# Three up bodies with 258 columns, the rest on rows of 256, and arrays on multiples of 512 bytes

## What is computed

```python
mod_x = (jax.nn.silu(c) @ w_mod[l] + b_mod[l])[:, None, :]
sh1, sc1, g1, sh2, sc2, g2 = jnp.split(mod_x, 6, axis=-1)
...
xs = xs + g2 * sq_relu_mlp(rms_norm(xs, norm_mlp_g[l]) * (1 + sc2) + sh2, mlp_w1[l], mlp_w2[l])

def rms_norm(x, g):
    y = xf * lax.rsqrt(jnp.mean(xf * xf, axis=-1, keepdims=True) + EPS)
    return (y * g.astype(F32)).astype(x.dtype)

def sq_relu_mlp(h, w1, w2):
    return jnp.square(jax.nn.relu(h @ w1)) @ w2
```

## Time and profile before

| | |
|---|---|
| median of 3 runs | 1370.04 us (1368.95 to 1371.89) |
| profiled execution | 1371.54 us, span of its core 1369.7 us |
| busy | PE 98%, PEld 93%, DVE 62%, ACT 51%, POOL 21% |
| mean granted clock of PE | 0.997 of full speed |
| HBM | 168 MB read, 124 GB/s over the span |

### The profile page before, as it was taken

How to read it: one execution, slowest core, us unless ns; L and a number is a source line. 1 busy time by engine, 2 the same in 40 slices (tenths; PEclk the granted TensorE clock), 3 DMA queues, 4 the chain that set the end, 5 groups by cost and what they waited for, 6 DMA issues and landing times.

```text
span 1369.7 us, 28118 instructions
## 1 busy us (share of the span) xinstructions
PE 1344.8 (98%) x11256; PEld 1269.9 (93%) x11256; DVE 854.4 (62%) x1308; ACT 701.6 (51%) x1135; POOL 287.9 (21%) x296
## 2 busy tenths in 40 slices
PE   6999999999999999999999999999999999999998
PEld 4899998988899999999999999999998988999998
DVE  4755789985455665543587666566736666765563
ACT  4468888878544455422533322333226665663553
POOL 2000224223566786621100000000020000200002
PEclk9999999999999999999999999999999999999999
DMA  9732232322401110123466565565423320656562
GB/s 327 201 87 85 79 92 78 94 78 77 139 33 34 61 33 32 63 78 101 139 193 193 184 194 190 185 192 182 134 93 123 98 74 32 192 175 204 173 194 78
DMA packets 138030, 170.88 MB, mean 125 GB/s; under 512 B 10912, under 2 KB 121760, under 8 KB 137920
## 3 DMA queue, kind: packets, MB, share of 16 engines
q1 hardware_dynamic: 137312, 169.13, 39.4%
q0 software_dynamic: 608, 0.19, 0.1%
HBM read 168.25 MB, written 1.05 MB: 124 GB/s over the span
## 4 chain that ended last, share of the span: by engine, by line
PE 84%; DVE 7%; ACT 4%; issue 2%; POOL 2%; DMA 1%; SPq 0%; DVEq 0%; ACTq 0%; POOLq 0%
PE bank L2531 54%; PE bank L2538 7%; PE bank L2945 3%; PE bank L2933 3%; DVE qkv L1721 2%; DVE w_lo L1655 2%; PE bank L2457 1%; PE bank L2962 1%; POOL qkv L768 1%; PE bank L3184 1%; PE bank L2887 1%; PE bank L3207 1%; PE bank L2911 1%; PE bank L2809 1%; DMA first_w<-in_w_mod 1%
## 5 line engine op out<-in xcount | busy, mean ns | idle before, releaser
L1655 DVE TENSOR_TENSOR w_lo<-raw,w_hi 128x1024 fp32r<-128x1024 f32 x214 | 267.3, 1250 | 308.9 <-ACT w_hi L915 308.4
L915 ACT ACTIVATE w_hi<-raw 128x1024 fp32r<-128x1024 f32 x214 | 225.5, 1055 | 378.0 <-PE bank L2531 376.0
L2531 PE MATMUL bank<-h_hi,w_hi 128*128 128x256 f32 x1472 | 300.0, 282 | 7.4 <-DVE w_lo L1655 4.9
L2531 PE MATMUL bank<-h_hi,w_lo 128*128 128x256 f32 x1472 | 292.8, 277 | 0.0
L2531 PE MATMUL bank<-h_lo,w_hi 128*128 128x256 f32 x1472 | 287.5, 278 | 0.0
L2531 PEld LDWEIGHTS bank<-h_hi,w_hi 128*128 128x128 f32 x1472 | 225.5, 188 | 18.1 <-issue 10.2
L2531 PEld LDWEIGHTS bank<-h_hi,w_lo 128*128 128x128 f32 x1472 | 225.1, 188 | 0.0
L2531 PEld LDWEIGHTS bank<-h_lo,w_hi 128*128 128x128 f32 x1472 | 222.0, 188 | 0.3 <-DVE h_lo L1914 0.2
L2531 PE MATMUL bank<-hid_hi,w_hi 128*128 128x256 f32 x768 | 173.5, 280 | 0.0
L2531 PE MATMUL bank<-hid_hi,w_lo 128*128 128x256 f32 x768 | 172.2, 278 | 0.0
L2531 PE MATMUL bank<-hid_lo,w_hi 128*128 128x256 f32 x768 | 172.2, 278 | 0.0
(11 more groups left out here) (363 smaller groups left out, 2484.7 us busy)
## 6 DMA issues: line engine op xcount, KB each, us to landing
raw<-in_mlp_w SPq DMA_DIRECT2D x128, 512.0 KB, 3.7
late_w<-in_w_mod SPq DMA_DIRECT2D x56, 512.0 KB, 4.4
raw<-in_even_w_in SPq DMA_DIRECT2D x48, 512.0 KB, 3.7
raw<-in_w_mod SPq DMA_DIRECT2D x24, 512.0 KB, 4.4
first_w<-in_w_mod SPq DMA_DIRECT2D x16, 512.0 KB, 10.8
raw<-in_even_w_out SPq DMA_DIRECT2D x16, 512.0 KB, 3.5
raw<-in_attn_w_qkv SPq DMA_DIRECT2D x16, 512.0 KB, 3.7
raw<-in_attn_w_o SPq DMA_DIRECT2D x8, 512.0 KB, 3.5
```

The source lines that it names most:

```text
L915: act.activation(stored(w_hi, j, four), raw[:, j % RAW], ACT.Copy).then_inc(hi_ready, 1)
L1655: dve.tensor_tensor(stored(w_lo, j, four), raw[:, j % RAW], stored(w_hi, j, four).bitcast(F32), ALU.subtract).then_inc(split_done, 1)
L2531: return pe.matmul(bank[2 * pair + t][:, c - n0:c - n0 + CTX], w_[:, k, t * P:(t + 1) * P], x_[:, c:c + CTX], start=(kk == 0 and first and ...
```

## The change

Three edits:

- `up_x`, `rooted_hi`, `rooted_lo` are new. DVE's `normal` makes x · gain · root for one feature tile in one of four buffers, ACT's `normal_high` adds the shift and rounds, and `normal_low` on DVE takes the rest. All eight tiles are made in bodies 0 and 1 of up10 (`NORMAL_IN` = 2), two with each pair.
- Bodies 0 to 2 of up10 (`ROOTLESS` = 3) go on with 258 columns of `up_hi`, `up_lo`, and are written out. Body 3 of up10 and all of up11 multiply `rooted_hi`, `rooted_lo`, 256 columns. There DVE's `positive` takes the maximum with 0 straight from the bank, and ACT only squares. PE waits once for the last `rooted_lo` ahead of body 3.
- `xT`, `raw`, `w_hi`, `w_lo`, and with them `w_hi2`, `w_lo2` and all that `F` places, start on multiples of 512 bytes. The small arrays lie ahead of them; `d_last` moves into `sp_x`.

```diff
+ALIGNED = 512
-SHIFT, UP_ROW = 2, 272
+SHIFT, UP_ROW, ROOTLESS, NORMAL_IN = 2, 272, 3, 2
...
+        base[0] = (base[0] + ALIGNED - 1) // ALIGNED * ALIGNED
+        xT = place("xT", [KT, T])
+        raw = place("raw", [RAW, UNIT_K, UNIT_C])
+        w_hi = place("w_hi", [SPLIT, UNIT_K, UNIT_C], F32R)
+        w_lo = place("w_lo", [SPLIT, UNIT_K, UNIT_C], F32R)
         mod_off = base[0]
...
+        up_x = F("up_x", 76, [4, T - CTX])
+        rooted_lo = F("rooted_lo", 80, [KT, T - CTX], F32R)
+        rooted_hi = F("rooted_hi", 88, [KT, T - CTX], F32R)
...
+                def normal_high(k):
+                    act.wait_ge(nrm["t"], 5 * KT + k + 1)
+                    act.activation(rooted_hi[:, k], up_x[:, k % 4], ACT.Identity, bias=modv[:, 1, 3, k, 1:2]).then_inc(nrm["high"], 1)
...
                 def body(it):
                     u = it * 2 * s["upp"] + s["unit"]
                     for pair in range(2):
                         split_hi(u + 4 + 2 * pair, 4 + 2 * pair, True)
-                        relus(it, pair)
-                        squares_of(it, pair)
+                        squares_alone(it, pair)
...
+            def positive(s, it, pair):
+                dve.wait_ge(hid_done, it * 4 + (s["up"] + 2 * pair + 2))
+                dve.sem_inc(act_waits, 1)
+                dve.wait_ge(slot_free, it * 2 * s["upp"] + (s["unit"] + (pair + 1) * s["upp"] + PRIME_SLOT))
+                for t in range(2):
+                    dve.tensor_scalar(relu[:, 2 * pair + t, 0:T - CTX], bank[2 * pair + t][:, 0:T - CTX], 0.0, None,
+                                      ALU.max).then_inc(evac_done, 1)
+
+            def normal(k):
+                dve.scalar_tensor_tensor(out=up_x[:, k % 4], in0=xT[:, k, CTX:T], scalar=gain[:, 1, 1, k, 1:2],
+                                         in1=n_rs[:, 0:T - CTX], op0=ALU.mult, op1=ALU.mult).then_inc(nrm["t"], 1)
+
+            def normal_low(k):
+                dve.wait_ge(nrm["high"], high_upto(turn["mlp1"], k) + KT)
+                dve.scalar_tensor_tensor(out=rooted_lo[:, k], in0=up_x[:, k % 4], scalar=modv[:, 1, 3, k, 1:2],
+                                         in1=rooted_hi[:, k].bitcast(F32), op0=ALU.add, op1=ALU.subtract).then_inc(nrm["lo"], 1)
...
+                def rootless_body(it):
+                    u = it * 2 * s["upp"] + s["unit"]
+                    for pair in range(2):
+                        k = 4 * it + 2 * pair
+                        if it < NORMAL_IN:
+                            normal(k)
+                            normal(k + 1)
+                        split_lo(u + 4 + 2 * pair, 4 + 2 * pair, True)
+                        rooted(s, it, pair)
+                        if it < NORMAL_IN:
+                            normal_low(k)
+                            normal_low(k + 1)
+                        split_lo(u + 5 + 2 * pair, 5 + 2 * pair, True)
+                        hidden_low(s, it, pair)
...
-                if n0 == 0 and (h is up_hi or h is up_lo):
+                if s["name"] in ("up10", "up11"):
                     kk = j % s["upp"] * UNIT_K + k
+                    n = T - CTX + (SHIFT if h is up_hi or h is up_lo else 0)
...
+                        first = 0
+                        if half == 0:
+                            first = ROOTLESS
+                            for n in range(1, ROOTLESS * per_body):
+                                unit(s_, n // per_body, n % per_body, up_hi, up_lo, 0, **(normed(nm) if n < per_body else {}))
+                            pe.wait_ge(nrm["lo"], high_upto(turn[nm], KT - 1) + KT)
+                        with nc.Fori(first, s_["bodies"], engines=[ENG.PE]) as it:
+                            for n in range(per_body):
+                                unit(s_, it, n, rooted_hi, rooted_lo, 0)
```

More of the change, by code:

```diff
@@ L207, in build @@
         vec = place("vec", [NVEC])
-        xT = place("xT", [KT, T])
-        raw = place("raw", [RAW, UNIT_K, UNIT_C])
-        w_hi = place("w_hi", [SPLIT, UNIT_K, UNIT_C], F32R)
-        w_lo = place("w_lo", [SPLIT, UNIT_K, UNIT_C], F32R)
         modv = place("modv", [2, 6, 8, 2])
@@ L1462, in squares_of, with squares_alone @@
                         act.activation(r_, r_, ACT.Square).then_inc(s_sq, 1)
+                def squares_alone(it, pair):
+                    for t in range(2):
+                        wait_alone(evac_done, it * 4 + (2 * s["pair"] + 2 * pair + t + 1 + PRIME_EVAC))
+                        r_ = relu[:, 2 * pair + t, 0:T - CTX]
+                        act.activation(r_, r_, ACT.Square).then_inc(s_sq, 1)
+                def normal_high(k):
[4 more added lines that the diff above has]
+                    for pair in range(2):
+                        split_hi(u + 4 + 2 * pair, 4 + 2 * pair, True)
+                        if it < NORMAL_IN:
+                            normal_high(4 * it + 2 * pair)
+                            normal_high(4 * it + 2 * pair + 1)
+                        relus(it, pair)
+                        squares_of(it, pair)
+                        split_hi(u + 5 + 2 * pair, 5 + 2 * pair, True)
+                        after(s, it, pair)
                 def body(it):
@@ L1476, in hidden @@
                     split_hi(s["unit"] + 3, 3, True)
-                with nc.Fori(0, s["bodies"], engines=[ENG.Activation]) as it:
+                    for it in range(ROOTLESS):
+                        rootless_body(it)
+                with nc.Fori(ROOTLESS if s["name"] == "up10" else 0, s["bodies"], engines=[ENG.Activation]) as it:
                     body(it)
@@ L2264, in body @@
                         split_lo(u + 4 + 2 * pair, 4 + 2 * pair, True)
-                        rooted(s, it, pair)
+                        positive(s, it, pair)
                         split_lo(u + 5 + 2 * pair, 5 + 2 * pair, True)
@@ L2272, in hidden @@
                     split_lo(s["unit"] + 3, 3, True)
-                with nc.Fori(0, s["bodies"], engines=[ENG.DVE]) as it:
+                    for it in range(ROOTLESS):
+                        rootless_body(it)
+                with nc.Fori(ROOTLESS if s["name"] == "up10" else 0, s["bodies"], engines=[ENG.DVE]) as it:
                     body(it)
@@ L3140, in _, with mlp @@
             segment(s_, *mix, mixed, 3)
-            def mlp(layer, last):
+            def mlp(layer):
                 nm, n0 = f"mlp{layer}", 0 if layer == 0 else CTX
-                x_ = (h_hi, h_lo, 0) if layer == 0 else (up_hi, up_lo, 0)
                 if layer:
-                    unit(SEG["up10"], 0, 0, *x_, **normed(nm))
+                    unit(SEG["up10"], 0, 0, up_hi, up_lo, 0, **normed(nm))
                 sumsq(nm, T - n0)
@@ L3151, in mlp @@
                     s_ = SEG[f"up{layer}{half}"]
-                    segment(s_, *x_, first=1 - half if layer else 0, late=layer == 0, **(normed(nm) if half == 0 else {}))
+                    per_body = 2 * s_["upp"]
+                    if layer == 0:
+                        segment(s_, h_hi, h_lo, 0, late=True, **(normed(nm) if half == 0 else {}))
+                    else:
+                        first = 0
[7 more added lines that the diff above has]
+                                unit(s_, it, n, rooted_hi, rooted_lo, 0)
                     for i in range(2 * layer):
```

9 lines of the change are left out of this document (4 added, 5 removed).

## The result

The changed kernel takes 1408.35 us (median of 5 runs, 1407.59 to 1408.51), the kernel before, on the same chip, 1371.89 (5 runs, 1368.95 to 1373.92). The ratio is 1.0262, with a 95% interval of 1.0251 to 1.0273. It was forecast at 1363 in a range of 1356 to 1370. What came is the second rival, slower everywhere, and at its size: 1406 was worked out for it.

The account below looks back on a forecast made before the run. PE's matmul spacing was taken to bound the kernel. Alignment and 256 columns gave -7.9 us, PE's wait +1.0, in sum -6.9: 1364.6 for the profiled execution, 1363 for the median, range 1356 to 1370.

Parts of the forecast that it names:

- second rival: All products: weights and moving rows at the same offset make everything slow, +36 us, 1406; chance 0.12 for all slower cases.
- slow level: Units with weights in `w_hi2`, `w_lo2`: 119.8 ns against 113.3, put down to starting 64 bytes past a 128-byte multiple.
- Layer 0: 0: Layer 0's products: no change, since `w_hi`, `w_lo` already lie on 128-byte multiples and run fast.
- down10 -1.9, up11 -2.95, down11 -1.8 and -0.3: Layer 1's MLP products: gains in us from alignment and 256 columns, priced at 113.3 ns a matmul.
- middle level: Spacing of 117.8 ns in which the first pair of weight buffers stays once a slow unit has disturbed it.
- first rival: Layer 1: slow units vanish but it stays at 117.8 ns, -1.3 us, 1368.7; chance 0.20 for all or half of layer 1.
- q and k -0.6: The q and k products: 25 slow and 94 middle matmuls become fast, -0.6 us.
- Bodies 0 to 2 of up10: 0: Up10's first three bodies: they keep 258 columns, so no change in time.
- Body 3: Up10's last 96 matmuls, now 256 columns: priced at 117.8 ns, -0.3 us.
- The ring: DVE and ACT in up10: turns of 6.8 us in four pairs with `up_x`, costing PE some +1.0 us; 5.39 without relu.
- third rival: All products: moving rows' offset also costs, spacing falls to at best 108.8 ns, 1330; chance 0.10 in part or whole.
- faster start: Wait for `first_w` at the start: aligned rows might shorten its DMA, -1.4 us; 0.54 covers the forecast with or without it.

Follow-up runs that it names:

- a3: Changed kernel with all that `F` places, moving rows among it, 64 bytes further, weights left on multiples of 512: 1385.28 us, ratio 1.0096.
- a4: Changed kernel with weights and moving rows both 64 bytes past a multiple of 512: 1408.68 us, ratio 1.0272.
- b1: Changed kernel with all weight buffers 128 and moving rows 64 bytes past a multiple of 512: 1371.4 us, ratio 0.9996.
- b2: Changed kernel with all weight buffers 64 bytes past a multiple of 512 and moving rows on one: 1368.68 us, ratio 0.9973.
- e2: Changed kernel with d4's order of work, weights 320 and moving rows 256 bytes past a multiple of 512: 1367.05 us, ratio 0.9963.
- d3: The kernel of b2 run once more, unchanged: 1373.22 us, ratio 1.0008.
- d4: The kernel of b2 with DVE making the next pair's `up_x` earlier, in its wait for ACT: 1370.69 us, ratio 0.999.
- e1: Changed kernel with d4's order of work, weights 128 and moving rows 64 bytes past a multiple of 512: 1367.45 us, ratio 0.9958.
- a2: Changed kernel with the arrays placed as in the kernel before: 1371.62 us, ratio 1.0003.
- c1: Kernel before (258 columns, loops) with weights 64 bytes past a multiple of 512 and moving rows on one: 1372.38 us, ratio 0.9998.
- a1: Kernel before with only the new placement, large arrays on multiples of 512 bytes: 1406.84 us, ratio 1.0253.

## Why the prediction was wrong, step by step

- **The reason of the slow level failed; all else follows.** "`w_hi2`, `w_lo2` 64 bytes past one. I take this as the reason of the slow level." In the rows, all slow units had two things in common, the weights' 64 bytes and the equal start, and I chose the one that made the change good. a3, a4 and b1, b2 show the other: weights at 64 are fast beside rows at 0 (b2), weights at 0 slow beside rows at 0 (after). The change put into every product the property that it should have taken out of one buffer.
- **Layer 0: 0** was the term that was off, by 32 us: layer 1's q product begins at 1079.00 us where it was 1046.98, and 3.3 us more are lost from there to up10. It hung on "on 128-byte multiples already and is fast".
- **down10 -1.9, up11 -2.95, down11 -1.8 and -0.3**: in the changed kernel +0.6, -0.4, +0.4. As the price of a placement at +64 they were right: 43.54, 43.52 and 38.10 us in e2 give -1.9, -2.95 and -1.8. Even there they hang on the level that the stretch falls into, which b1 (45.23, 45.23, 39.58) shows and the sum didn't allow for.
- **The middle level as the wake of a slow unit** was wrong: a3, b1 and d3 have it with no slow unit anywhere, and the kernel before has it in layer 0, ahead of any. The first rival (1368.7) had b1's down10 and up11 right (45.23 each), for another reason than it gave; that b2's median is 1368.68 is luck, since b2's down10 and up11 are fast.
- **q and k -0.6**: lost with the rest. **Bodies 0 to 2 of up10: 0** was right, 120.7 to 121.1 ns wherever PE doesn't wait. Body 3 was in the middle level in d4, e1 and e2 (117.8), as priced, and at 120.0 in the changed kernel.
- **The ring was right**: turns of 6.8 us (6.79), of 6.0 without `up_x` (5.99 in a2 and d4), and room for 43.5 in up11 with ACT's relu gone. PE's wait was put at 1.0 us; the pauses over 121 ns at the starts of up10's units add up to 1.4 us in the changed kernel and 1.6 in a2. The forecast's lower bound was reckoned wrongly: with 0.7 us for two `up_x` its own sum leaves 3.2 - 5 x 0.19 - 4 x 0.7 = -0.6, so a wait of 0.6 us and not none.
- **Relu on ScalarE and code without a loop, 0 each**: nothing in the rows speaks against it; c1's up10 with loops and d4's without are 43.50 and 43.22 us for 360.
- **The third rival** (down to 108.8 ns) is excluded as far as these kernels go: the lowest level of a long stretch is 113.3 in all. The Trainium skill ("TensorE: Matmul & The Clock Gate", section "Back-to-back issue gap") gives N / 2.4 + 2.5 ns, 109 for 256 columns, for a matmul by itself, and says that in a stream of weight loads and matmuls both set the spacing. No stretch of these runs with 256 columns and weight loads comes down to 109. **The faster start** (-1.4) didn't come either: the chain waits as long for `first_w` as before, in the changed kernel

```profile
5.61 12.93 DMA first_w<-in_w_mod
```

- **The second rival** was worked out right, at 36 us (37.0 measured), and got too small a chance, 0.12 together with all else that is slower. Its evidence ("in every slow unit weights and moving rows lie at the same place within 512 bytes (64 past), in every fast one at different places") was as good as that of the forecast. What I held against it, that `up_hi`'s rows change their distance with each tile and have about 120 ns throughout, was misread: the spacing does change with the tile. In up11, from the starts of its matmuls, the four tiles of a unit have 120.0, 119.0, 121.0 and 123.3 ns in a1, where the first is at distance 0, and 123.5, 120.0, 119.0 and 120.8 in c1, where the first is at +64: nearly the same four numbers, moved on by one tile, as the distance is. Any four tiles go through all four distances, so the mean is 120.8 in both. For these rows the tile at +64 is the slowest.
- **The chances** of "faster" (0.54 + 0.08 + 0.07) have no term for the 0.10 of "faster everywhere" as the list gives it. It changes nothing in the forecast.

## What to carry to other kernels

Where a matmul loads weights each time, look at the distance between the weights' and the moving rows' places in SBUF, modulo 256 bytes: for 256 columns here 64 bytes ahead is best of the seven distances tried and none is worst, 6 to 7 ns of 113. Placing every array on a multiple of 512 bytes gives all the same start and so the worst distance. Even at the best one the level isn't certain from one execution to the next, so a difference of 0.3% between two kernels like these wants more than one session. When all slow cases share two properties, try the cheapest run that parts them (one number in `free` was enough here) before a change rests on one of them. And put work that an idle engine has to do into its wait, not ahead of the step that others wait for, even if it is only 0.8 us a turn: four turns of it cost PE 1.4.

## What the runs showed of the hardware

- A stretch with weight load and 256 columns of fp32r in each matmul runs in one of a few steady spacings, the same to 0.1 ns in all kernels: 113.3, 116.7, 117.3, 117.8, 118.3, 118.7 and 120.0 ns. Which of them can occur goes by the distance modulo 256 bytes; at +64, +96, +128 and -64 there are two.
- Once entered, a spacing lasted through loops to the end of the stretch, up to 720 matmuls. What picks it at the start stays open: it was seen to differ between kernels with one placement (b1 and e1, c1 and b2) and between two executions of one kernel (b2 and d3), whose medians were 4.5 us apart.
- 258 columns in rows of 1088 bytes have 120.7 to 121.1 ns on average in all placements, where 256 columns with the same weights have 113.3 at best. Within a unit they go from 119 to 124 ns by the tile's distance modulo 256, which is lowest at -64 and highest at +64 (a1, c1). Whether the columns or the change of distance from tile to tile keep them from 113.3 wasn't parted.
